# Encoder layer on one core: memory keys computed in halves between self-attention steps, the depthwise convolution on VectorE alone

## The chip, the cores and the metric

One core of a Trainium2 chip runs one program. The metric is device time in microseconds (us) of one execution; lower is better. The engines are TensorE (PE: matmuls and transposes), VectorE (DVE), ScalarE (ACT), GpSimd (POOL) and SyncE (SP), whose queue issues the loads. They work at the same time and wait for each other through semaphores.

## The reference

Two sequences, 256 and 512 tokens of width 1024, go through one encoder layer with shared weights, in fp32. What matters here is the first half:

```
h = layer_norm(x);  m = layer_norm(mem)                    # mem: 256 rows per sequence
q, k, v, a, gate = split(h @ w_in)                         # 512, 128, 128, 512, 512 columns
q, k = rope(rms_norm(q)), rope(rms_norm(k))                # per head of 64; 8 q heads, 2 kv heads
att  = softmax(q @ k.T / 8) @ v                            # within each sequence
u    = depthwise_conv31(a * sigmoid(gate)) + bias          # along tokens, 512 channels
u    = silu(layer_norm(u))                                 # over channels
h    = layer_norm(2**0.25 * h + concat(att, u) @ w_mix)
xa   = softmax((h @ w_cq) @ (m @ w_ck).T / 16) @ (m @ w_cv) @ w_co     # 4 heads of 256
h    = layer_norm(2**0.25 * h + xa)
```

A mixture of experts (32 experts, two per token) and a last norm follow; the change doesn't touch them.

## The kernel before

The 768 tokens lie as six tiles of 128 rows in `hres`; transposed, channels on partitions, in `hT`. Each engine has its own instruction list, written out by hand, and runs it in order. PSUM has eight banks; `plan_banks` gives every result its bank and its turn, in four banks for products ("mm"), two for transposes ("tr") and two for attention values ("pv"). `full` waits until a bank is written, `was_read` and `claim` until it is free again.

Weights come in slabs of 512 columns (2 MB) in the order of `weight_slabs`, through `ring`, which has three slots: slab n is loaded into slot n % 3 once the last product with slab n - 3 has been done (`load_slab`, L466). The order is a, g, q, kv, mix0, mix1, ck0, ck1, cv0, cv1, cq0, cq1, co0, co1.

- **Start.** Norm of the six tiles: VectorE takes statistics (`dve_stats`, L640), GpSimd the coefficients and the gain (`pool_coef`, `pool_gain`, L625), ScalarE the normalised rows (`act_hat`, L632), VectorE the bias (`dve_bias`, L657). TensorE transposes them (`rows_T`, L1577).
- **Convolution input.** `gates(c, s)` on TensorE makes a and gate for 128 channels c and sequence s, `gate(c, s)` on ScalarE evicts them, the sigmoid at L938.
- **Convolution.** The 256-token sequence: ScalarE scales one shifted copy per tap (L964), GpSimd adds it (L762). The 512-token sequence: VectorE alone, one instruction per tap (L1197), 31 taps for each of four groups of 128 channels. Mean and variance over channels are matmuls with a matrix of 1/512 (L1641); square root, reciprocal (L1216), scaling and Silu (L1017) follow, all before self-attention.
- **q, k, v.** Six tiles; squares and their sums on ScalarE, the factors on GpSimd (L746), the rotation (`rotate`, L666 to L682) on VectorE for four tiles and on GpSimd for two; TensorE transposes q and k (L1617).
- **Self-attention** is a loop of 24 steps (`STEPS`), each one query tile with two heads: eight steps with 256 keys, then sixteen with 512. Per step: scores (TensorE, L1707), maximum (VectorE, L1257), two exponentials with their sums (ScalarE, L1065), reciprocal (VectorE), normalisation of the two rows of probabilities (GpSimd, L778), transposes (TensorE, L1718), two copies out (VectorE, L1276). The values (L1730) come once per pair of heads, over all its query tiles.
- **Output projection and memory.** `product` (L1568) is eight matmuls. The mix products of six tiles (mix0 and mix1) are interleaved with norm 1, the transposes of the new rows, and the four memory tiles, which are loaded, normed and transposed here. Then come the keys of the memory (ck0, ck1: eight products of 512 columns), its values (cv0, cv1: eight products), the queries of cross-attention, cross-attention, and the rest.

## Time and profile before

| | us |
|---|---|
| median of 3 runs (lowest, highest) | 1152.93 (1151.47, 1153.18) |
| profiled execution | 1157.94 |
| its span, first to last instruction | 1156.2 |
| TensorE busy in the span | 978.5 (85%), mean granted clock 0.918 |
| VectorE, ScalarE, GpSimd busy | 427.1, 272.6, 424.6 |

A span is what the trace covers of one execution; "busy" counts instructions at work, not waits. The granted clock is the share of TensorE's full clock of 2.4 GHz; 0.50 is its lower level, 1.2 GHz. The chain of waits is followed back from the last instruction, at each step to what released it. L1568 is line 1568 of the kernel before. A matmul of fp32 leaves two records, so the counts of matmuls in the trace are twice those of the code.

### The profile page before, as it was taken

What the parts mean: (1) busy time and instruction counts of PE and PEld (TensorE: products, weight loads), DVE (VectorE), ACT (ScalarE), POOL (GpSimd) and SP (SyncE); (2) the same over time, 40 slices, a digit from 0 to 9 for tenths busy, and PEclk for the clock granted to TensorE, in tenths of its full rate; (3) what the DMA queues carried; (4) which work ended last, traced back from release to release, by engine and by line L of the source; (5) the groups of instructions that cost most, each with busy time, mean ns of one, the idle gap of its engine ahead of it and who ended that gap; (6) DMA issues with size and microseconds to landing.
All of it is one profiled execution on the core that took longest, in us unless ns stands there. A gap on an engine that the chain in (4) does not pass through costs nothing.

```text
span 1156.2 us, 10290 instructions
## 1 busy us (share of the span) xinstructions
PE 978.5 (85%) x3368; PEld 509.1 (44%) x3368; DVE 427.1 (37%) x702; ACT 272.6 (24%) x647; POOL 424.6 (37%) x496
## 2 busy tenths in 40 slices
PE   4899884757779998999999999995897999999910
PEld 3465442433334453444555754554643444444300
DVE  5199999566541432000000332225241112111156
ACT  2444564254421221001111430112010111111111
POOL 6688889727751542000000441120115121212037
PEclk9899997769989998999999999996598999999965
DMA  9201200120003014220420005006299799999652
GB/s 325 97 1 32 77 0 1 35 75 1 1 1 109 19 59 142 73 73 0 145 73 0 1 30 243 37 37 272 94 369 394 302 420 421 414 393 418 233 223 109
DMA packets 46234, 166.15 MB, mean 144 GB/s; under 512 B 8515, under 2 KB 13891, under 8 KB 33893
## 3 DMA queue, kind: packets, MB, share of 16 engines
q1 hardware_dynamic: 39460, 152.88, 34.3%
q0 software_dynamic: 6720, 12.60, 2.9%
q8 instruction: 28, 0.46, 0.2%
q14 instruction: 26, 0.20, 0.0%
HBM read 157.92 MB, written 18.03 MB: 152 GB/s over the span
## 4 chain that ended last, share of the span: by engine, by line
PE 68%; DVE 17%; POOL 8%; issue 4%; DMA 2%; ACT 1%; POOLq 0%; SPq 0%; DVEq 0%
PE ps L1568 34%; DVE cat L1197 11%; PE ps L1895 7%; PE ps L1924 7%; PE ps L1898 5%; POOL scr L778 4%; PE ps L1730 2%; PE ps L1654 2%; PE ps L1872 2%; PE ps L1679 2%; POOL hres L625 2%; PE ps L1577 1%; PE ps L1827 1%; PE ps L1718 1%; PE ps L1641 1%
## 5 line engine op out<-in xcount | busy, mean ns | idle before, releaser
L778 POOL TENSOR_SCALAR scr<-scr,rinv 128x256 f32<-128x256 f32 (+1 forms) x72 | 86.1, 1208 | 258.1 <-DVE rinv L1223 215.6
L1568 PE MATMUL ps<-ring,hT 128*128 128x512 f32 (+1 forms) x384 | 152.5, 558 | 23.3 <-ACT cat L990 12.9
L1568 PE MATMUL ps<-hT,ring 128*128 128x512 f32 (+1 forms) x512 | 170.7, 497 | 1.7 <-ACT hT L929 1.0
L1568 PEld LDWEIGHTS ps<-hT,ring 128*128 128x128 f32 x512 | 99.7, 195 | 71.4 <-issue 62.0
L1197 DVE SCALAR_TENSOR_TENSOR cat<-early,cpar,cat 128x512 f32<-128x512 f32 x120 | 127.5, 1063 | 4.2
L762 POOL TENSOR_TENSOR cat<-cat 128x256 f32<-128x256 f32 x120 | 114.1, 951 | 29.8 <-ACT cat L964 13.4
L1568 PEld LDWEIGHTS ps<-ring,hT 128*128 128x128 f32 x384 | 74.6, 196 | 98.8 <-issue 78.7
L1239 DVE TENSOR_REDUCE nmax<-ps 128x1 f32<-128x256 f32 x24 | 10.2, 424 | 215.3 <-PE ps L1654 215.3
L841 POOL DMA_INDIRECT pair_rows<-hT,sidx x22 | 22.0, 1001 | 182.9 <-DVE hT L1492 182.0
L1568 PE MATMUL ps<-ring,cat 128*128 128x512 f32 x192 | 83.8, 593 | 0.9 <-ACT cat L1055 0.9
L614 POOL TENSOR_SCALAR lnt<-mv 128x1 f32<-128x1 f32 x28 | 14.5, 518 | 161.0 <-DVE mv L642 160.0
L964 ACT ACTIVATE cat<-early,cpar 128x256 f32<-128x256 f32 x120 | 57.5, 506 | 43.2 <-POOL cat L762 42.7
L1924 PE MATMUL ps<-ring,memx 128*64 128x512 f32 (+1 forms) x144 | 59.9, 610 | 0.7 <-DVE memx L1482 0.7
L1568 PE MATMUL ps<-scr,ring 128*128 128x512 f32 x128 | 57.9, 616 | 0.7 <-ACT scr L1081 0.7
L1291 DVE SCALAR_TENSOR_TENSOR hres<-hres,ps 128x512 f32<-128x512 f32 x24 | 16.4, 685 | 109.3 <-PE ps L1568 109.3
L1482 DVE COPY memx<-ps 128x256 f32<-128x256 f32 x22 | 9.3, 424 | 128.4 <-PE ps L1907 124.6
L1568 PEld LDWEIGHTS ps<-ring,cat 128*128 128x128 f32 x192 | 35.9, 190 | 43.8 <-issue 43.8
L1568 PE MATMUL ps<-ring,scr 128*128 128x512 f32 x128 | 55.1, 592 | 0.0
L625 POOL TENSOR_TENSOR hres<-hres,gb 128x1024 f32<-128x1024 f32 x20 | 48.8, 2444 | 7.2 <-ACT hres L632 7.1
L632 ACT ACTIVATE hres<-hres,lnc 128x1024 f32<-128x1024 f32 x20 | 24.8, 1240 | 105.5 <-POOL lnc L616 105.3
L1718 PE MATMUL ps<-ident,scr 128*128 128x128 f32 x160 | 28.4, 304 | 21.3 <-POOL scr L778 20.3
L657 DVE TENSOR_TENSOR hres<-hres,gb 128x1024 f32<-128x1024 f32 x20 | 28.6, 1437 | 44.4 <-POOL hres L625 44.4
(267 smaller groups left out, 1447.2 us busy)
## 6 DMA issues: line engine op xcount, KB each, us to landing
ring<-w_down SPq DMA_DIRECT2D x16, 1024.0 KB
early<-w_gate SPq DMA_DIRECT2D x12, 1024.0 KB, 9.5
early<-w_up SPq DMA_DIRECT2D x12, 1024.0 KB, 13.0
ring<-w_gate SPq DMA_DIRECT2D x10, 1024.0 KB
ring<-w_up SPq DMA_DIRECT2D x10, 1024.0 KB
scr<-w_down SPq DMA_DIRECT2D x8, 1024.0 KB
cat<-w_down SPq DMA_DIRECT2D x8, 1024.0 KB
scr<-w_gate SPq DMA_DIRECT2D x5, 1024.0 KB
```

The source lines that it names most:

```text
L625: nc.gpsimd.tensor_tensor(rows, rows, g, ALU.mult).then_inc(ln_gain, 1)
L632: nc.scalar.activation(rows, rows, ACT.Identity, bias=lnc[:, n % 2, 1:2], scale=lnc[:, n % 2, 0:1]).then_inc(ln_hat, 1)
L657: nc.vector.tensor_tensor(rows, rows, b, ALU.add).then_inc(ln_done, 1)
L762: g.tensor_tensor(acc[:, c, 0:length], acc[:, c, 0:length], tap[n % NTAP], ALU.add).then_inc(conv_done[0], 1)
L778: g.tensor_scalar(prob[u % 4][:, 0:width], prob[u % 4][:, 0:width], rinv[:, u % 4:u % 4 + 1], None, ALU.mult).then_inc(prob_ready, 1)
L964: a.activation(tap[n % NTAP], src, ACT.Copy, scale=cpar[:, c, k:k + 1]).then_inc(taps_ready, 1)
L1197: ins = v.scalar_tensor_tensor(out=dst, in0=src, scalar=cpar[:, c, k:k + 1], in1=dst, op0=ALU.mult, op1=ALU.add)
L1568: last = t.matmul(out_of(bank), lhs(k), rhs(k), start=(k == 0), stop=(k == KC - 1))
L1718: last = t.transpose(bank[:, c * P:(c + 1) * P], prob[u % 4][:, c * P:(c + 1) * P], ident[:, :])
L1895: last = t.matmul(gu_out(64 * h, 64 * h + 64, b), xT[b][:, k, 64 * h:64 * h + 64], gu_of(n % GU_SLOTS, k), start=(k == 0), stop=(k == KC - 1))
L1898: last = t.matmul(gu_out(0, P, b), xT[b][:, k, :], gu_of(EXPERT_BLOCKS[j][1] % GU_SLOTS, k), start=(k == 0), stop=(k == KC - 1))
L1924: last = t.matmul(ps[h0:h1, 2 + n, :], hidT[b][:, k, h0:h1], w[:, k, n * 512:(n + 1) * 512], start=(k == 0), stop=(k == 1))
```

## The change

- **Memory.** Loads, norm and transposes of the four memory tiles move to the start, between the gates (`LN_M` now follows `LN_X`). The transposed memory lies in two halves, `mT[0]` and `mT[1]`.
- **Memory keys.** The eight key products are cut in halves of four matmuls (`memory_keys`), sixteen pieces, and one is issued in each of the steps listed in `CK_AT` of the self-attention loop. The slabs ck0 and ck1 are loaded ahead of mix0 and mix1.
- **Convolution.** VectorE alone, both sequences in one row of 798 columns with zeros between them (`AW`): 124 instructions. 108 stand ahead of the self-attention loop, 16 in its first four steps. Mean, variance, scaling and Silu move into the loop (`MEAN_AT`, `VAR_AT`).
- **Rotation.** Nine instructions on VectorE for all six tiles, with tables that hold the signs; two tiles ahead of the last channel group, two behind its first 15 taps, two in the loop.
- **Self-attention.** ScalarE normalises the probabilities (`self_normal`) in place of GpSimd, and does the second of the two copies (`self_turned`); the values come every second step for two query tiles (256 columns) in place of all at once.
- **Norm 1** is no longer interleaved with the memory's norms; GpSimd and VectorE take each tile's gain and bias before the next tile. Its gain and bias vectors have their own tile, `gb1`.

The core of the diff:

```diff
+            ("ck0", w_ck[:, 0:512]), ("ck1", w_ck[:, 512:1024]),
             ("mix0", w_mix[:, 0:512]), ("mix1", w_mix[:, 512:1024]),
-            ("ck0", w_ck[:, 0:512]), ("ck1", w_ck[:, 512:1024]),
             ("cv0", w_cv[:, 0:512]), ("cv1", w_cv[:, 512:1024]),
...
+QKV_ORDER = [("q", 0), ("q", 1), ("kv", 0), ("kv", 1)] + [(what, i) for i in range(2, NT) for what in ("q", "kv")]
 S_AHEAD = 3
 STEPS = len(SELF) // 2
-STEP_LAST = {SELF[2 * k][0]: k for k in range(STEPS)}
+GQ = 2 * P
+QKT_AT = {3: (2, 3), 6: (4, 5)}
+CK_AT = {k: n for n, k in enumerate((0, 1, 2, 3, 4, 5, 6, 7, 9, 11, 13, 15, 17, 19, 24, 25))}
+MEAN_AT, VAR_AT = 10, 14
...
+            for i in range(2):
+                sp.dma_start(mrow[i], mem[i * P:(i + 1) * P, :]).then_inc(mem_in[i], 16)
...
             for i in range(2, MT):
                 full(sp, ("mT", i - 2, 1))
                 sp.dma_start(mrow[i % 2], mem[i * P:(i + 1) * P, :]).then_inc(mem_in[i % 2], 16)
-            for n in range(7, 9):
+            for n in range(3, 8):
                 load_slab(n)
-            sp.wait_ge(ln_done, LN_1[-1] + 1)
+            sp.wait_ge(conv_out, CC)
+            for j in range(2):
+                sp.dma_start(gb1[:, j, :], bcast(lnp[2 + j])).then_inc(gb1_in, 16)
+            for n in range(8, 13):
+                load_slab(n)
             load_gb(2)
-            for n in range(9, len(w_slabs)):
+            for n in range(13, len(w_slabs)):
...
             norms(LN_X)
+            norms(LN_M[0:2])
...
+            norms(LN_M[2:MT])
...
+            for i in range(NT):
                 factors(i)
...
-            normalise(SELF, 0, True)
-            norms(sorted(LN_1 + LN_M))
-            normalise(CROSS, STEPS, False)
+            norms(LN_1, lag=0)
...
+            act_hat(act, LN_M[0])
             gate(0, 1)
...
+            act_hat(act, LN_M[1])
+            gate(1, 0)
+            for i in range(2):
+                mem_T(i)
+            gate(1, 1)
+            act_hat(act, LN_M[2])
+            act_hat(act, LN_M[3])
+            gate(2, 0)
+            for i in range(2, MT):
+                mem_T(i)
+            gate(2, 1)
+            for s in range(2):
+                gate(CC - 1, s)
...
+            def self_normal(k):
+                act.wait_ge(inv_ready, k + 1)
+                for u in (2 * k, 2 * k + 1):
+                    width = SELF[u][4]
+                    a.activation(sprob[u % 4][:, 0:width], sprob[u % 4][:, 0:width], ACT.Copy,
+                                 scale=rinv[:, u % 4:u % 4 + 1]).then_inc(prob_ready, 1)
+            def self_turned(k):
+                n, s, h, i, width = SELF[2 * k + 1]
+                key, m = ("sT", 2 * k + 1), width // P
+                bank = full(act, key)
...
+            qk_T(0)
+            qk_T(1)
             for k in range(STEPS + 3):
                 if k < STEPS:
                     self_exps(k)
...
+                if 1 <= k <= STEPS:
+                    self_normal(k - 1)
+                if 2 <= k < STEPS + 2:
+                    self_turned(k - 2)
+                if k >= 4 and k % 2 == 0:
+                    group_out((k - 4) // 2)
...
+                if CK_AT.get(k, 0) % 2 == 1:
+                    c = CK_AT[k] // 2
+                    if c == 0:
+                        act.wait_ge(u_ready, CC)
+                    bank = full(act, ("ck", c))
+                    a.activation(kmT[c], bank, ACT.Copy).then_inc(free(("ck", c)), 1)
+                if k == MEAN_AT + 1:
+                    for s, (t0, length) in enumerate(SEQS):
+                        was_read(act, ("mean", s))
...
+                if k == VAR_AT:
+                    for s in range(2):
+                        full(act, ("var", s))
+                    for s, (t0, length) in enumerate(SEQS):
+                        bank = full(act, ("var", s))
+                        a.activation(cstd[:, t0:t0 + length], bank[:, 0:length], ACT.Sqrt,
+                                     bias=epsv[:, 0:1]).then_inc(free(("var", s)), 1)
+                if VAR_AT + 3 <= k < VAR_AT + 3 + CC:
+                    c = k - VAR_AT - 3
+                    act.wait_ge(conv_norm, CC)
+                    a.activation(catv[:, CC + c, :], normed[:, c, :], ACT.Silu, bias=cpar[:, c, TAPS + 2:TAPS + 3],
+                                 scale=cpar[:, c, TAPS + 1:TAPS + 2]).then_inc(conv_out, 1)
...
+            def glu(c):
+                for s, (t0, length) in enumerate(SEQS):
+                    was_read(dve, ("a", c, s))
+                    was_read(dve, ("g", c, s))
+                    gated = upad[:, c, CONV_AT[s] + PAD:CONV_AT[s] + PAD + length]
+                    last = v.tensor_tensor(gated, gated, sig[:, c % 2, t0:t0 + length], ALU.mult)
+                last.then_inc(u_ready, 1)
+            def conv(c, k0, k1):
+                for k in range(k0, k1):
+                    src = upad[:, c, k:k + AW]
                     if k == 0:
...
+                        dve.wait_ge(u_ready, c + 1)
+                        ins = v.tensor_scalar(acc[:, c, :], src, cpar[:, c, 0:1], cpar[:, c, TAPS:TAPS + 1],
+                                              ALU.mult, ALU.add)
                     else:
...
+                        dve.wait_ge(conv_done, c * TAPS + k)
+                        ins = v.scalar_tensor_tensor(out=acc[:, c, :], in0=src, scalar=cpar[:, c, k:k + 1],
+                                                     in1=acc[:, c, :], op0=ALU.mult, op1=ALU.add)
+                    ins.then_inc(conv_done, 1)
+            def rotate(i):
+                pos = i - SEQS[TILES[i][0]][0] // P
+                r = raw[i].rearrange("p (h d) -> p h d", h=NQK)
+                dve.wait_ge(rqk_ready, i + 1)
+                rs = rqk[:, i, 1, :].rearrange("p (h a) -> p h a", a=1).to_broadcast([P, NQK, HD])
+                link(v.tensor_tensor(r, r, rs, ALU.mult))
+                A, B = rtmp
+                for tabx, h0, h1 in ((qtab, 0, HEADS), (ktab, HEADS, NQK)):
+                    last = v.tensor_tensor(A[:, h0:h1, :], r[:, h0:h1, :],
+                                           tabx[:, 0, pos:pos + 1, :].to_broadcast([P, h1 - h0, HD]), ALU.mult)
+                    for m in range(2):
+                        t = tabx[:, 1, pos:pos + 1, m:HD:2].to_broadcast([P, h1 - h0, HD // 2])
+                        last = v.tensor_tensor(B[:, h0:h1, m:HD:2], r[:, h0:h1, 1 - m:HD:2], t, ALU.mult)
+                link(last)
+                qo = raw[i][:, 0:HEADS * HD].rearrange("p (c a d) -> p a c d", c=PAIRS, a=2)
+                v.tensor_tensor(qo, A[:, 0:HEADS, :].rearrange("p (a c) d -> p a c d", a=2),
+                                B[:, 0:HEADS, :].rearrange("p (a c) d -> p a c d", a=2), ALU.add)
+                v.tensor_tensor(r[:, HEADS:NQK, :], A[:, HEADS:NQK, :], B[:, HEADS:NQK, :],
+                                ALU.add).then_inc(rot_ready, 1)
+            mem_rows(LN_M[0:2])
+            for n in LN_M[0:2]:
+                dve_bias(dve, n, link)
+            was_read(dve, "cpar")
+            glu(0)
+            conv(0, 0, 12)
+            mem_rows(LN_M[2:MT])
+            conv(0, 12, 18)
+            for n in LN_M[2:MT]:
+                dve_bias(dve, n, link)
+            conv(0, 18, 22)
+            glu(1)
+            conv(0, 22, TAPS)
+            conv(1, 0, 16)
+            glu(2)
+            conv(1, 16, TAPS)
+            conv(2, 0, 6)
+            glu(3)
+            conv(2, 6, TAPS)
             dve.wait_ge(tabs_ready, 1)
...
+            was_read(dve, ("mT", MT - 1, 1))
+            rotate(0)
+            rotate(1)
+            conv(3, 0, 15)
+            rotate(2)
+            rotate(3)
...
             for k in range(STEPS + 2):
                 if k < STEPS:
...
                     pair_inverse(k - 1)
                 if k >= 2:
                     pair_turned(k - 2)
+                if k < 4:
+                    conv(3, 15 + 4 * k, 19 + 4 * k)
+                elif k < 6:
+                    rotate(k)
+                if k == MEAN_AT + 1:
+                    for s, (_, length) in enumerate(SEQS):
+                        mean, at = full(dve, ("mean", s)), CONV_AT[s]
+                        for c in range(CC):
+                            last = v.tensor_tensor(acc[:, c, at:at + length], acc[:, c, at:at + length],
+                                                   mean[:, 0:length], ALU.subtract)
+                        last.then_inc(free(("mean", s)), 1)
+                if k == VAR_AT + 1:
+                    for s in range(2):
+                        was_read(dve, ("var", s))
+                    link(v.reciprocal(cstd, cstd))
+                if k == VAR_AT + 2:
+                    for s, (t0, length) in enumerate(SEQS):
+                        at = CONV_AT[s]
+                        for c in range(CC):
+                            last = v.tensor_tensor(normed[:, c, t0:t0 + length], acc[:, c, at:at + length],
+                                                   cstd[:, t0:t0 + length], ALU.mult)
+                            if s == 1:
+                                last.then_inc(conv_norm, 1)
...
+            for i, n in enumerate(LN_1):
+                if i >= 1:
+                    dve_bias(dve, LN_1[i - 1], link)
+                for j in range(2):
+                    residual(("mix", i, j), i, j).then_inc(free(("mix", i, j)), 1)
+                    was_read(dve, ("mix", i, j))
                 dve_stats(dve, n, link)
...
+            dve_bias(dve, LN_1[-1], link)
...
+            gates(1, 0)
+            for i in range(2):
+                rows_T("m", i, mrow[i], LN_M[i])
+            gates(1, 1)
+            gates(2, 0)
+            for i in range(2, MT):
+                rows_T("m", i, mrow[i % 2], LN_M[i])
+            gates(2, 1)
+            for s in range(2):
+                gates(CC - 1, s)
...
+            def memory_keys(n):
+                c, half = divmod(n, 2)
+                bank = claim(("ck", c)) if half == 0 else ps[:, place[("ck", c)][0], :]
+                w = slab(f"ck{c // 4}")
+                for k in range(4 * half, 4 * half + 4):
+                    last = t.matmul(bank, w[:, k, c % 4 * P:(c % 4 + 1) * P], mT[half][:, k % 4, :],
+                                    start=(k == 0), stop=(k == KC - 1))
+                if half == 1:
+                    done(("ck", c), last)
...
             for k in range(STEPS + 3):
+                if k == SEQS[0][1] // P * PAIRS:
+                    for key in ("qT", "kT", "kv"):
+                        was_read(pe, (key, NT - 1))
                 if k < STEPS:
                     self_scores(k)
                 if 2 <= k < STEPS + 2:
                     self_turn(k - 2)
...
+                if k >= 4 and k % 2 == 0:
+                    self_values((k - 4) // 2)
+                for i in QKT_AT.get(k, ()):
+                    qk_T(i)
+                if k in CK_AT:
+                    memory_keys(CK_AT[k])
+                if k == MEAN_AT:
+                    channel_mean("mean")
+                if k == VAR_AT:
+                    channel_mean("var")
```

## Rows read from the trace of the kernel before

**Rows 1.** Busy time by stage: start:end, length, busy us of each engine, granted clock, DMA share, GB/s.

```profile
58.70:196.40 137.70, 115.34 (x330) 64.46 (x329) 133.37 (x127) 70.05 (x222) 117.97 (x121) 0.93 0.08 23
196.40:249.30 52.90, 31.57 (x108) 20.18 (x106) 33.28 (x74) 20.44 (x64) 26.60 (x42) 0.78 0.15 40
249.30:347.77 98.47, 74.19 (x353) 34.58 (x353) 51.92 (x96) 37.34 (x105) 64.02 (x48) 0.88 0.03 11
347.77:442.10 94.33, 90.09 (x256) 43.11 (x257) 31.91 (x50) 19.71 (x26) 36.81 (x39) 0.99 0.24 84
```

**Rows 2.** The chain of waits, 340 to 660 us: start, us, what.

```profile
347.77 34.57 PE ps L1568 x80
...
421.05 0.87 PE ps L1577 x8
...
442.10 112.84 PE ps L1568 x256
```

**Rows 3.** DMA issues, 425 to 500 us: KB each, median us to landing.

```profile
ring<-w_cv SPq DMA_DIRECT2D x2, 2048.0 KB, 7.7
```

**Rows 4.** Timeline of DVE, ACT and POOL: start, us, instruction, idle before it.

```profile
23.20 1.24 DVE L657 TENSOR_TENSOR hres<-hres,gb 128x1024 f32<-128x1024 f32 x1 [2.24 <-POOL hres L625]
...
56.42 0.60 ACT L938 ACTIVATE scr<-ps 128x512 f32<-128x512 f32 x1 [6.27 <-PE ps L1568]
...
365.47 1.24 ACT L632 ACTIVATE hres<-hres,lnc 128x1024 f32<-128x1024 f32 x1 [17.96 <-POOL lnc L616]
...
366.86 2.36 POOL L625 TENSOR_TENSOR hres<-hres,gb 128x1024 f32<-128x1024 f32 x1
```

**Rows 5.** The convolution taps on DVE, one source line: duration in ns, min/median/max.

```profile
L1197 DVE SCALAR_TENSOR_TENSOR cat<-early,cpar,cat x120: 752/1097/1304, 58.7 to 195.4; 128x512 f32<-128x512 f32 x120
```

**Rows 6.** Timeline of DVE and POOL, 183 to 192 us.

```profile
183.53 8.39 DVE L1197 SCALAR_TENSOR_TENSOR cat<-early,cpar,cat 128x512 f32<-128x512 f32 x10
...
187.58 2.49 POOL L746 TENSOR_TENSOR rqk<-rqk,mhalf 128x10 f32<-128x10 f32 x1
```

**Rows 7.** Groups of DVE, 0 to 360 us, by shape: busy us, mean ns | idle before.

```profile
L1257 DVE TENSOR_REDUCE nmax<-ps 128x2 f32<-128x1024 f32 x16 | 19.5, 1218 | 12.2 <-PE ps L1707 12.2
...
L1216 DVE RECIPROCAL scr<-scr 128x768 f32<-128x768 f32 x1 | 5.0, 4952 | 0.5 <-ACT scr L1013 0.5
...
L650 DVE SCALAR_TENSOR_TENSOR hres<-hres,mv,gb 128x1024 f32<-128x1024 f32 x2 | 2.6, 1284 | 3.0 <-DMA gb<-lnp 3.0
L1209 DVE TENSOR_TENSOR cat<-cat,ps 128x512 f32<-128x512 f32 x4 | 2.5, 679 | 0.0
...
L666 DVE TENSOR_TENSOR ring<-ring,rqk 128x640 f32<-128x640 f32 x2 | 1.6, 820 | 5.6 <-POOL rqk L747 5.6
```

**Rows 8.** Timeline of PE in self-attention, 292 to 300 us.

```profile
293.03 3.65 PE L1730 MATMUL ps<-scr,early 128*64 128x512 f32 x16
296.61 1.13 PE L1707 MATMUL ps<-early 64*128 64x512 f32 x4
297.67 1.09 PE L1718 MATMUL ps<-ident,scr 128*128 128x128 f32 x8
```

**Rows 9.** Timeline of ACT, 231 to 301 us.

```profile
231.64 1.28 ACT L1013 ACT_TABLE_LOAD   x1
232.94 0.47 ACT L1013 ACTIVATE scr<-ps,epsv 128x256 f32<-128x256 f32 x1
...
242.90 3.78 ACT L1017 ACTIVATE cat<-cat,cpar 128x768 f32<-128x768 f32 x4 [4.78 <-DVE cat L1218]
...
299.12 0.69 ACT L1065 ACTIVATE scr<-ps,nmax 128x512 f32<-128x512 f32 x1 [1.80 <-DVE nmax L1257]
...
300.37 0.20 ACT L1065 ACTIVATION_READ_ACCUMULATOR scr<-ps,nmax 128x1 f32 x1
```

**Rows 10.** Busy time in two stretches of 4 us (columns as in rows 1).

```profile
316.00:320.00 4.00, 1.94 (x12) 1.14 (x12) 2.32 (x5) 2.18 (x7) 4.00 (x3) 1.00 0.00 0
...
336.00:340.00 4.00, 2.98 (x12) 1.80 (x10) 1.34 (x3) 0.00 (x0) 2.62 (x2) 0.50 0.00 0
```

515 lines of the change are left out of this document (186 added, 329 removed).

## The prediction, made before the changed kernel ran

> **What bounds the kernel now.** I read the busy time by stage first [rows 1]. From 58.7 to 196.4 us VectorE is busy 133 of 137.7 us (the taps of the 512-token sequence), while TensorE has 22 us to spare. From 196.4 to 347.8 us nothing is full: TensorE works 32 of 53 and then 74 of 98 us, at granted clocks of 0.78 and 0.88, and in the second of these stretches GpSimd works 64 of 98 us, normalising the softmax rows. From 347.8 us TensorE works 90 of 94 us. Second, the chain of waits [rows 2] is TensorE alone from there on, through output projection, memory keys and memory values. So TensorE's work after 347.8 us is paid at full price, and the same work before it is free as far as it fits into idle time. The sum needs two numbers: what leaves the full stretch, and how much later that stretch begins.
>
> **What leaves the full stretch.** A product is eight matmuls of 512 columns; the five products of the piece at 347.77 take 34.57 us (two records each matmul), so 6.9 us [rows 2]. Before, the time from 347.77 to the end of the value products is 94.33 (output projection, eight transposed tiles, a wait at the end) [rows 1] + 112.84 (keys and values) [rows 2] = 207.2 us. After, there remain 12 output products (82.8), four transposed tiles of 0.87 (3.5) [rows 2] and 8 value products (55.2): 141.5. The slab cv1 now goes into the slot of mix0, so its load is issued when the last mix0 product ends; TensorE then still has one transposed tile and one product, 7.8 us, and a slab takes 7.7 us to land [rows 3] plus about 0.5 us to issue: a wait of 0.5 to 2.5, I take 1. The key product's eight evictions and the memory norms leave this stretch too, but lay beside TensorE and are worth nothing. Gain: 207.2 - 142.5 = 64.7 us. Norm 1 becomes a serial loop on VectorE and GpSimd (residual, statistics, coefficients, hat, gain, bias: about 9.6 us by the durations in [rows 4]); a tile's two products take 13.8, so it stays hidden. Cross-attention and experts issue the same work; nothing is taken there.
>
> **The first tap comes later.** ScalarE ends the sigmoid of tile (0,1) at 57.0 us. Behind it in the new order stands the hat of memory tile 1 (1.24), then GpSimd's gain (2.36), VectorE's bias (1.24), and only then the gating of both sequences (about 0.4 more) [rows 4]: +5.3, first tap at 63.2 instead of 57.9. The memory loads join the queue behind the first two slabs, VectorE waits there until 57 us anyway: nothing. The rope tables and two memory gains now run on GpSimd beside the taps.
>
> **The taps.** A 512-wide tap takes 1097 ns in the median but 752 ns at least [rows 5]; the short ones are those from 183.5 us on, where GpSimd, until then adding taps, works on 10 numbers per partition [rows 6]. The same instruction 1024 wide takes 1284 [rows 7]. Between those, 798 columns take 752 + 286 x (1284-752)/512 = 1049 ns, and 0.036 to the next: 1.085 us. With GpSimd idle for nearly all of this stretch I take the fast price; at the slow ratio (1097/752) it would be 1.53 us. Before the loop: 104 taps (112.8), four openers (3.8), three more gatings (3.5), statistics and bias of two memory tiles (5.7), and four rotations. A rotation is nine instructions; by the 0.82 of its 640-wide scaling [rows 7] and the 0.4 to 0.7 that 256 to 512 columns cost, 4.3 us, so 17.2. GpSimd's tables and gains, some 10 us, slow taps by 3.5. Sum 146.5: the loop's first maximum at 209.8. TensorE has finished q, k and v by 186 (it starts them at about 124: the gates plus 4 us of transposes, then six tiles at 10.3), so VectorE is last here.
>
> **Steps 0 to 7 (256 keys).** VectorE: maximum 0.7, reciprocal 0.15, one copy 0.4 and four taps or one rotation (4.3): 5.6 us, six times less a bit at the start, 33: 242.8. TensorE per step: scores and transposes about 1.1, values 0.4, a key piece of four matmuls 3.45: 5.0, hidden. Steps 6 and 7 have no taps left, so TensorE's two key pieces set the pace: 11 us. TensorE idles from about 196 to 210 and restarts at half clock: 1.3. The exponentials of step 8 start at 255.
>
> **Steps 8 to 23 (512 keys).** Per step TensorE needs scores 1.07, transposes 1.09, values 1.8 every second step [rows 8], VectorE a maximum of 1.22 [rows 7], ScalarE two exponentials (1.45 with their sums) and now the normalisation: one activation of 512 columns takes 0.69 and 768 columns 3.78/4 = 0.945 [rows 9], so two take 1.4; and one copy, 0.6. The loop closes over two steps: exponentials 1.45, normalise 1.4, copy (frees the bank) 0.6, second half of the transposes 0.7, key piece 3.45, scores 1.1, maximum 1.3: 10.1 us for two steps when a key piece lies in them, 8.4 or ScalarE's 7.8 when none does. Thrown between: mean and variance sums on TensorE, 5.2 each; mean subtraction 4.4, reciprocal 4.95 [rows 7] and scaling 4.4 on VectorE; squares 3.0, roots 1.2, four Silus 4.0 and ten table loads on ScalarE. Walking the queues with these, the exponentials start at 265 (step 10), 278 (12, after the mean), 288 (14), 299 (15, variance and roots), 305 (16), 311 (17, reciprocal and scaling), 319, 326, 334, 341 (18 to 21, a Silu and two loads in each), 346 and 350 (23). So of some 45 us thrown in, 22 reach the path. Tail: exponentials and normalisation 2.9, transposes, values 1.8, two key pieces 6.9 and the last values, 16: 366. At half clock TensorE's work costs double. It kept full clock through the short waits of 316 to 320 us and ran at 0.50 behind the long one before 336 [rows 10]; beside the Silus its waits in the new order are 3 to 5 us, between the two. Nothing lost is one bound; the other is half clock from step 22 on to the mix, some 16 us of work that lies on the path. I take 6: transposes, values and scores of step 22 (3.9) and 2 in the tail. Mix begins at 372, 24 us later than before.
>
> Table loads: each took 1.28 us, and the root behind the one at 231.64 started at once, at 232.94 [rows 9]; that is what the walk uses. The Trainium skill, "ScalarE: Activation LUTs", section "What ACT_TABLE_LOAD costs", counts 1283 ns and a drain of about 1380 ns for every switch of table set, and advises calling functions set by set; this change interleaves Silu with Exp. By that, ten loads would cost some 14 us more; the trace of before shows no such drain, and the row decides.
>
> **The sum.** -64.7 + 24 = -41. The profiled execution took 1157.9 (span 1156.2), 5 above the median of 1152.9; I take the difference off the median: **1112 us**.
>
> **Rivals.** *The loop pipelines better (A):* clock held, key pieces under the pair's slack at 9.5: mix at 358 to 362, 1098 to 1102. For it: TensorE at full clock in most of self-attention. Against: one bank of each half for transposes. *ScalarE becomes the bound (B):* it has 1.45 + 1.4 + 0.6 of a 4 us step, plus loads, squares and roots; a pause behind each of ten loads as long as the load itself (13), 0.2 to 0.3 us of hand-over in each of 24 steps (5 to 7), or half clock to the end (10 more): 1120 to 1132. For the pause speaks only the drain that the Trainium skill's "ScalarE: Activation LUTs" adds to each switch; no row of before shows one. *Other side (C):* the 798-wide taps cost the slow price because something besides GpSimd's adding slows them. 120 x 0.48 = 58 us, all on VectorE's path: 1170. It decides from 0.34 us more per tap (1.39 us) on. For it: the median of the 120 taps is the slow price. Against: the ten fast ones beside busy ScalarE and TensorE. Halfway, it is also how the change could do nothing.
>
> **How the numbers follow.** My case 0.58 (1102 to 1120), A 0.15, B 0.20, C 0.07, of which 0.02 falls within 0.2% (about what a measurement of this kernel can tell from no change). Faster 0.93, same 0.02, slower 0.05. The range takes my case, A and B with their bounds: 1096 to 1132.
>
> **What would show it.** Taps 798 wide at about 1.05 us; the first maximum of self-attention near 210 us; key pieces between steps; eleven table loads in self-attention, 1.28 each with no gap behind; the output projection starting near 372; 142 us from there to the end of the value products, with a wait of about 1 us for cv1. Wrong if taps stay above 1.3 us, if ScalarE's steps run over 5.5 us without a key piece, or if the mix starts beyond 400.

## The result, and the profile after

The changed kernel takes 1106.07 us (median of 4 runs, 1104.72 to 1110.7) where the kernel before takes 1152.65 in runs beside it (1151.47 to 1153.18): 46.6 us less, a ratio of 0.9586 with a 95% interval of 0.9564 to 0.9608 (the two medians alone give 0.9596). The forecast was 1112, range 1096 to 1132. The profiled execution took 1107.07 with a span of 1105.4, 50.8 less than the span before; of the 5 us by which the profiled execution before lay above its median, only 1 is left here.

Busy time by stage, changed kernel (columns as in [rows 1]). The first row starts at 63.20, where the first tap was forecast; the others start where the loop's first exponential and the exponentials of steps 8, 16 and 23 do, and the last ends where the output projection starts:

```profile
63.20:201.90 138.70, 129.05 (x399) 73.54 (x397) 134.96 (x157) 30.95 (x159) 33.56 (x30) 0.99 0.18 57
201.90:251.66 49.76, 41.08 (x148) 19.11 (x148) 31.58 (x57) 21.05 (x67) 0.00 (x0) 0.86 0.01 4
...
251.66:301.71 50.05, 48.89 (x214) 24.30 (x212) 23.11 (x35) 32.74 (x69) 0.00 (x0) 1.00 0.14 39
301.71:345.82 44.11, 32.50 (x152) 16.25 (x148) 17.44 (x31) 38.22 (x67) 0.00 (x0) 0.88 0.07 24
345.82:363.69 17.87, 14.62 (x64) 7.49 (x65) 2.17 (x5) 6.82 (x14) 0.00 (x0) 0.90 0.08 19
```

Set beside [rows 1], self-attention is no longer a place where nothing is full. VectorE is full to 201.9 as before; then TensorE works 41 of 50 and 49 of 50 us; from step 16 to 23 (301.71 to 345.82) ScalarE is the full one, 38 of 44 us, and TensorE falls to 0.88 of its clock; in the tail everything waits in line.

The chain of waits of the changed kernel from the output projection on:

```profile
363.69 34.57 PE ps L1595 x80
...
442.97 61.97 PE ps L1595 x144
...
591.57 3.69 PE ps L1670 x16
```

And the start of cross-attention in the kernel before:

```profile
641.58 3.69 PE ps L1654 x16
```

The output projection starts at 363.69, 15.9 us later than before [rows 2]. From there to the end of the value products (442.97 + 61.97 = 504.94) are 141.25 us in place of 207.2: 65.9 less. Cross-attention starts at 591.57 in place of 641.58, 50.0 earlier, and the rest keeps that. So the result is 65.9 - 15.9 = 50.0 by the two profiles.

### The profile page after: what moved, and what is told of

The parts are those of the page before. It is cut to its first block, busy times and chain, and to the rows that moved or that the text cites. A ratio compares the mean times of both kernels' runs of the same rounds, so it can differ in the third digit from the quotient of the medians.

```text
span 1105.4 us, 10066 instructions
## 1 busy us (share of the span) xinstructions
PE 966.3 (87%) x3432; PEld 506.6 (46%) x3432; DVE 413.9 (37%) x680; ACT 260.2 (24%) x607; POOL 229.2 (21%) x296
## 4 chain that ended last, share of the span: by engine, by line
PE 61%; DVE 4%; ACT 3%; issue 3%; POOL 3%; DMA 1%; POOLq 0%; DVEq 0%
PE ps L1595 27%; PE ps L1942 8%; PE ps L1971 7%; PE ps L1945 5%; PE ps L1670 2%; PE ps L1919 2%; PE ps L1695 2%; PE ps L1874 1%; PE ps L1743 1%; POOL hres L644 1%; PE ps L1754 1%; PE ps L1604 1%; PE ps L1839 1%; DMA hT<-h_rows,gidx 1%; POOL slot_table L845 1%
## 5 line engine op out<-in xcount | busy, mean ns | idle before, releaser
L1595 PE MATMUL ps<-ring,hT 128*128 128x512 f32 (+1 forms) x384 | 145.6, 540 | 0.9 <-issue 0.9
L1182 DVE SCALAR_TENSOR_TENSOR cat<-early,cpar,cat 128x798 f32<-128x798 f32 x120 | 130.4, 1087 | 3.9
L651 ACT ACTIVATE hres<-hres,lnc 128x1024 f32<-128x1024 f32 x20 | 24.8, 1241 | 136.2 <-POOL lnc L635 135.9
L746 POOL TENSOR_SCALAR memx<-memx,rinv 128x256 f32<-128x256 f32 x24 | 22.1, 924 | 154.0 <-DVE rinv L1237 154.0
L1271 DVE TENSOR_REDUCE nmax<-ps 128x2 f32<-128x1024 f32 (+1 forms) x24 | 25.1, 1045 | 63.6 <-PE ps L1720 62.3
L1942 PE MATMUL ps<-early,hT 128*64 128x512 f32 x128 | 44.3, 627 | 0.8 <-ACT hT L1100 0.8
L1731 PE MATMUL ps<-ident,hT 128*128 128x128 f32 x160 | 26.4, 301 | 19.4 <-ACT hT L1015 17.7
L1945 PE MATMUL ps<-early,hT 128*128 128x512 f32 x96 | 42.5, 596 | 0.0
L1942 PE MATMUL ps<-ring,hT 128*64 128x512 f32 x96 | 42.3, 594 | 0.0
L1107 ACT ACTIVATE memx<-ps 128x256 f32<-128x256 f32 x22 | 8.4, 383 | 142.4 <-PE ps L1942 78.7
L1604 PE MATMUL ps<-ident,hres 128*128 128x128 f32 x144 | 22.5, 309 | 21.2 <-DVE hres L672 16.0
## 6 DMA issues: line engine op xcount, KB each, us to landing
ring<-w_down SPq DMA_DIRECT2D x16, 1024.0 KB, 16.9
early<-w_gate SPq DMA_DIRECT2D x12, 1024.0 KB, 10.6
```

The source lines that it names most:

```text
L651: nc.scalar.activation(rows, rows, ACT.Identity, bias=lnc[:, n % 2, 1:2], scale=lnc[:, n % 2, 0:1]).then_inc(ln_hat, 1)
L1182: ins = v.scalar_tensor_tensor(out=acc[:, c, :], in0=src, scalar=cpar[:, c, k:k + 1], in1=acc[:, c, :], op0=ALU.mult, op1=ALU.add)
L1271: v.tensor_reduce(nmax[:, c:c + 2], ps[:, b:b + 2, 0:width], AX.X, ALU.max, negate=True).then_inc(max_ready, 1)
L1595: last = t.matmul(out_of(bank), lhs(k), rhs(k), start=(k == 0), stop=(k == KC - 1))
L1604: last = t.transpose(bank[:, c * P:(c + 1) * P], rows[:, (4 * j + c) * P:(4 * j + c + 1) * P], ident[:, :])
L1731: last = t.transpose(bank[:, c * P:(c + 1) * P], sprob[u % 4][:, c * P:(c + 1) * P], ident[:, :])
```

## The experiments

Each experiment edits the changed kernel and is timed against the kernel before on its own chip. The third column is its ratio less 0.9586, times 1152.65: the difference from the changed kernel. Each ratio is uncertain by 0.002 to 0.003, so such a difference by 3 to 4 us. The span of the one profiled execution (1105.4 for the changed kernel) and the start of its output projection (363.69) stand beside it as a second witness. That witness varies too: the loop starts at 201.9 in the changed kernel, and at 202.7 to 203.0 in the profiles of e1, e2, e6 and e12 and at 205.7 in that of e8, whose edits all lie behind that start; and behind the projection, where only e4 differs, e6 and e9 took 2.5 and 1.8 us less.

| run | ratio (95%) | against the changed kernel, us | span | projection starts |
|---|---|---|---|---|
| e1 Silus in step 17 | 0.9532 (0.9514 to 0.9551) | -6.2 | 1100.5 | 358.48 |
| e12 Silus in step 18 | 0.9554 (0.9534 to 0.9574) | -3.7 | 1100.6 | 358.47 |
| e2 last key pieces earlier | 0.9504 (0.9484 to 0.9524) | -9.5 | 1096.5 | 354.99 |
| e3 hat first | 0.9554 (0.9532 to 0.9577) | -3.7 | 1101.2 | 359.92 |
| e4 keys after the projection | 0.9920 (0.9904 to 0.9935) | +38.5 | 1144.9 | 348.38 |
| e5 GpSimd busy beside taps | 0.9744 (0.9712 to 0.9776) | +18.2 | 1121.2 | 379.63 |
| e6 GpSimd normalises | 0.9527 (0.9497 to 0.9556) | -6.8 | 1096.3 | 357.08 |
| e7 taps split | 0.9608 (0.9577 to 0.9639) | +2.5 | 1106.0 | 364.62 |
| e8 TensorE filled | 0.9598 (0.9573 to 0.9623) | +1.4 | 1108.9 | 367.18 |
| e9 taps alternated | 0.9547 (0.9525 to 0.9568) | -4.5 | 1096.2 | 356.35 |
| e10 five edits | 0.9364 (0.9345 to 0.9384) | -25.6 | 1081.4 | 340.01 |
| e11 e10, normalisation split | 0.9385 (0.9370 to 0.9399) | -23.2 | 1079.1 | 336.76 |

My theory was that of the prediction: the key products leave the full stretch at full price and pay a part of it back in the loop. The rivals: the gain comes from the other parts, or the pieces are free in the loop.

**e4, the keys undone alone**

```diff
-CK_AT = {k: n for n, k in enumerate((0, 1, 2, ..., 24, 25))}
+CK_AT = {}
...
+            for n in range(2 * KC):      # behind the mix products
+                memory_keys(n)
             wv = [slab("cv0"), slab("cv1")]
```

> Memory keys undone alone: all eight key products behind the output projection again, slabs in the old order (mix before ck); convolution, rotation, normalisation and conv norm stay as changed. Nothing is left out. Theory (the prediction's steps 1, 4, 5): 55.2 us go back into the full stretch; the loop gives back 3 to 4 us in steps 6 and 7, 1.7 us for each of six pairs of steps, 7.3 in the tail, and perhaps 3 of half clock: 20 to 25 less there; so 30 to 35 us over the changed kernel, 1136 to 1141, with the output projection starting at 339 to 344. The keys are then worth some 33 of the 46.6 us and the rest of the change 13. Rival 1: the pieces were hidden but for the tail: 48 us more (1154, as slow as the kernel before: the keys are the whole gain). Rival 2: the loop pays the pieces in full: no more than 5 us over (the gain comes from the other parts).

38.5 us more, between theory and rival 1. The chain of waits of this kernel shows the keys back at full price:

```profile
348.38 34.57 PE ps L1600 x80
...
434.52 54.93 PE ps L1759 x128
489.45 54.95 PE ps L1600 x128
```

The other side is the start of the projection: 348.38, only 15.3 us earlier than with the pieces in the loop, not 20 to 25. Busy time of this kernel from the loop's first exponential to those of steps 8, 16 and 23, and to the projection:

```profile
202.02:241.88 39.86, 23.95 (x98) 13.00 (x100) 31.38 (x57) 18.86 (x63) 0.00 (x0) 0.60 0.00 0
241.88:293.38 51.50, 41.42 (x186) 21.19 (x182) 23.31 (x35) 32.24 (x67) 0.00 (x0) 0.90 0.00 1
293.38:336.47 43.09, 27.71 (x136) 14.08 (x132) 17.25 (x31) 37.77 (x65) 0.00 (x0) 0.80 0.08 25
336.47:348.38 11.91, 7.77 (x49) 4.69 (x49) 2.17 (x5) 6.22 (x13) 0.00 (x0) 0.86 0.00 1
```

Beside the changed kernel's 49.8, 50.1, 44.1 and 17.9 us, the eight pieces of steps 0 to 8 cost 9.9 us, the two of steps 16 to 23 cost 1.0 and the two of the tail 6.0. The four of steps 8 to 16 cost nothing: without them that stage is 1.5 us longer, though the theory had put 1.7 us on each pair of steps. In their place TensorE waits there, in step 11 for VectorE's subtraction of the mean, and does what stands behind the wait more slowly (these values take 1.95 us at full clock):

```profile
259.32 1.12 PE L1725 MATMUL ps<-early 64*128 64x512 f32 x2 [2.36 <-DVE cat L1311]
...
265.61 3.32 PE L1748 MATMUL ps<-hT,early 128*64 128x256 f32 x16
```

With less to do, TensorE had a lower granted clock in every stage: 0.60, 0.90, 0.80 and 0.86, against 0.86, 1.00, 0.88 and 0.90 with the pieces. How much of each stage the clock made up, and how much the other engines, is not shown. So, with the rest of the change in place, the keys are worth some 38 of the 46.6 us, and all the other parts together about 8.

**e6, normalisation undone alone**

```diff
-                if 1 <= k <= STEPS:
-                    self_normal(k - 1)
...
+            for k in range(STEPS):       # GpSimd
+                pool.wait_ge(inv_ready, k + 1)
+                for u in (2 * k, 2 * k + 1): ...  # g.tensor_scalar(..., rinv, None, ALU.mult)
```

> Normalisation of self-attention undone alone: GpSimd multiplies the rows by the reciprocals again, as in the kernel before (1562 ns for 512 columns, 924 for 256, against 715 and some 450 on ScalarE). Nothing is left out. Theory: a pair's normalisation is on the loop of two steps, so 3.12 instead of 1.32 us and a hand-over of 0.2 cost 2 us in each of eight pairs of steps, and some 0.5 in the steps of 256 keys where TensorE is not full; ScalarE gets back 1.3 us in each of the four Silu steps, which it paces: +16 + 2 - 5, so 8 to 15 us over the changed kernel, 1114 to 1121. Rival 1: ScalarE is the bound of the whole loop, and relief of it wins: 5 us or more less. Rival 2: GpSimd works beside, no change.

The theory falls: 6.8 us less, not 8 to 15 more. Stages of this kernel, from step 8 to 16 and from 16 to 23:

```profile
251.38:301.09 49.71, 48.79 (x214) 24.28 (x212) 23.10 (x35) 23.61 (x53) 23.58 (x16) 1.00 0.14 39
301.09:339.06 37.97, 30.14 (x152) 14.76 (x148) 17.68 (x31) 29.61 (x52) 21.99 (x14) 0.96 0.09 28
```

Steps 8 to 16 take 49.7 us whether a pair of rows is normalised in 1.3 us by ScalarE or in 3.1 by GpSimd. TensorE is busy all but 1 us in both, and the longer normalisation is hidden there. Steps 16 to 23 shrink from 44.1 to 38.0: ScalarE set the pace there, and it is relieved of 1.3 us a step. Putting the normalisation on ScalarE is thus a part of the change that cost time, as rival 1 had it, but in the last third of the loop only.

**e1 and e12, the Silus in one step**

```diff
-                if VAR_AT + 3 <= k < VAR_AT + 3 + CC:
-                    c = k - VAR_AT - 3
+                if k == 17:              # e12: 18
                     act.wait_ge(conv_norm, CC)
+                    for c in range(CC):
...
```

> The four Silus run together in step 17 instead of one each in steps 17 to 20; nothing is left out. Two of the eight table loads that the Silus bring remain, so ScalarE loses 6 x 1.28 = 7.7 us of work. Theory: in the changed kernel's profile ScalarE alone paces steps 17 to 21 (the chain of waits goes from table load to Silu to table load to exponential without a break), so most of it comes back: 5 to 7 us less than the 1106.1 of the changed kernel, about 1100. Rival 1: TensorE's key pieces of steps 17 and 19 take over as the pace at once: 0 to 2 us less. Rival 2: each change of table set costs a drain beside the load, which the profile doesn't show as such; then six changes less are worth 6 x 2.66 = 16 us (1090).

> The four Silus in step 18 instead of step 17, everything else as in the changed kernel; nothing is left out. With them in step 17, TensorE stood for 4.96 us behind them and came back at half clock: the key piece of step 19 took 5.75 instead of 3.6 us, and steps 19 to 20 were 8.9 us apart. Theory: in step 18 the Silus stand beside a step whose transposes and key piece TensorE can do without waiting for ScalarE, so the wait is shorter, the piece takes 3.6 us, and the 2.2 us and some more come back: 7 to 10 us below the changed kernel, 1096 to 1099. Rival: the wait only moves; 5 to 6 us below, as in step 17.

What they go at, the chain of waits of the changed kernel in step 17 and 18:

```profile
310.42 0.29 ACT L1063
310.70 1.01 issue
311.71 1.03 ACT cat L1063
312.75 1.28 ACT L1006
314.08 0.55 issue
314.63 0.86 ACT hT L1006 x3
```

That is a table load, a Silu, a table load and the exponential, with nothing between them. e1 came out as the theory had it: six loads less are worth 6.2 us (4.9 by the spans). e12 was to win more, and did not; its projection starts at the same time to 0.01 us. TensorE in e1, then in e12 (timelines, behind the Silus):

```profile
319.99 2.12 PE L1732 MATMUL ps<-ident,hT 128*128 128x128 f32 x8 [4.96 <-ACT hT L1016]
321.90 5.75 PE L1755 MATMUL ps<-scr,ring 128*128 128x512 f32 x8
```

```profile
324.43 2.12 PE L1732 MATMUL ps<-ident,hT 128*128 128x128 f32 x8 [3.68 <-ACT hT L1016]
326.48 3.48 PE L1744 MATMUL ps<-hT,early 128*64 128x256 f32 x16
```

In step 17 the key piece behind the wait took 5.75 in place of 3.6; in step 18 the piece was through before, and the transposes and values behind the wait took 2.12 and 3.48 in place of 1.09 and 1.95. The wait moved, and what came behind it paid for it, as the rival said. The two ratios lie too close to be told apart.

**e2, the last two key pieces in steps 21 and 23**

```diff
-... 17, 19, 24, 25))}
+... 17, 19, 21, 23))}
```

> The last two key pieces go into steps 21 and 23 instead of 24 and 25; nothing is left out. Theory: behind the last exponentials everything is serial (3.90 and 3.44 us of key pieces lie on the chain there), while TensorE is idle for 2 to 4 us in each of steps 20 to 23 behind ScalarE; so the tail loses 7.3 us and the steps gain some 1 to 2: 5 to 6 us less than the changed kernel, about 1101. Rival: the pieces push scores and transposes of steps 21 to 23 back by as much as they free at the end: 0 to 2 us less.

9.5 us less, more than expected. Its last two stages (exponentials of steps 16 to 23, then to the projection):

```profile
302.26:344.37 42.11, 35.28 (x161) 17.07 (x158) 17.23 (x31) 38.01 (x66) 0.00 (x0) 0.92 0.08 26
344.37:354.99 10.62, 9.06 (x57) 5.29 (x55) 2.18 (x5) 6.82 (x14) 0.00 (x0) 1.00 0.55 198
```

The tail went from 17.9 to 10.6, the 7.3 of two pieces. The steps did not pay for it: they became 2 us shorter, with the granted clock at 0.92 and 1.00 in place of 0.88 and 0.90. That the clock is what shortened them agrees with e4, but was not tried by itself.

**e3, the hat of memory tile 1 ahead of gate (0,1)**

```diff
             act_hat(act, LN_M[0])
-            gate(0, 1)
             act_hat(act, LN_M[1])
+            gate(0, 1)
```

> ScalarE's hat of memory tile 1 goes ahead of the gate (0,1); nothing is left out. Theory: the bias of that tile, at 57.05 us, is what VectorE waits for ahead of the first gating and tap; the sigmoid it needs is ready at 53.3. So first tap some 4 to 5 us earlier (56 instead of 60.7), and since VectorE is full from there to the loop's first maximum, the same 4 to 5 off the total, about 1102. Rival: TensorE, which ends its q, k, v products at 187 us, or the transposes behind the rotations, takes over and the loop starts as late as before: nothing off.

The first tap starts at 55.69 in place of 60.69, the loop 3.3 earlier, the total 3.7 lower. VectorE gave some of the 5 us back at 80.77: it now waits 3.99 us for GpSimd's gain of memory tile 2, and its first bias, beside the next gain, takes 3.28 us in place of 1.2. The changed kernel lost 4.1 us at the same place, in two taps beside these gains (see e5).

**e5, GpSimd busy beside the taps**

```diff
+            spare = qT[:, 0, 0:256]
+            link(g.memset(spare, 0.0))
+            for n in range(60):
+                link(g.tensor_tensor(spare, spare, spare, ALU.add))
             for i in range(NT):
                 factors(i)
```

> GpSimd gets 60 adds of 128x256 on a tile that nobody reads, behind the memory gains and ahead of the rotation factors: work without use, nothing is left out. In the kernel before, GpSimd's adds of this shape took 968 ns, so it is busy for some 58 us from about 84 us on; the factors are needed at 171 us, so nothing waits for them. Theory (the prediction's step 3): GpSimd's adding is what makes VectorE's taps slow (1097 against 752 ns, a ratio of 1.46); the taps beside it take 1.53 us instead of 1.05, VectorE loses 58 x (1 - 1/1.46) = 18 us and the total rises by as much, to about 1124. Rival (C): something else made them slow; the taps stay at 1.05 and the total within 2 us of the changed kernel.

18.2 us more, as the theory had it, but not by its arithmetic. The taps of this kernel that start from 100 to 139.5 us (min/median/max), and GpSimd's adds:

```profile
L1186 DVE SCALAR_TENSOR_TENSOR cat<-early,cpar,cat x29: 1279/1281/1395, 100.0 to 139.5; 128x798 f32<-128x798 f32 x29
```

```profile
L742 POOL TENSOR_TENSOR early<-early 128x256 f32<-128x256 f32 x60 | 71.1, 1185 | 4.7
```

A tap beside an add takes 1.28 us, 0.23 over the 1.05 without, not 1.53: the surcharge is not a ratio. And the adds ran longer than I assumed, 71 us in place of 58. By the profiles the loop starts 16.9 us later: 12.0 us are in the taps, 3.9 in the gatings, biases and openers beside the adds, and 1.1 came ahead of the first tap, where nothing was edited.

The Trainium skill, "SBUF — State Buffer", section "SBUF: two separate sides", calls the port pair that VectorE and GpSimd share an exclusive lock that is held for a whole instruction, so that the other blocks fully. The adds show contention, but not that much of it: between 84 and 156 us VectorE was busy 70.4 and GpSimd 67.7 of 72 us. A tap came every 1.31 us (15 in 19.72) and an add every 1.26 (60 in 75.75); in turns, a tap of 1.05 and an add of 0.97 (its time in the kernel before, beside shorter taps) would need 2.02. Longer GpSimd instructions come nearer to it. In the changed kernel two taps stand beside GpSimd's gains of memory tiles 2 and 3, 1024 columns wide (such a gain takes 2.35 us where VectorE is idle):

```profile
78.88 3.25 DVE L1182 SCALAR_TENSOR_TENSOR cat<-early,cpar,cat 128x798 f32<-128x798 f32 x1
82.17 3.01 DVE L1182 SCALAR_TENSOR_TENSOR cat<-early,cpar,cat 128x798 f32<-128x798 f32 x1
```

```profile
78.94 5.40 POOL L644 TENSOR_TENSOR memx<-memx,scr 128x1024 f32<-128x1024 f32 x2
```

These two taps took 2.2 and 2.0 us more than a tap alone, nearly the length of a gain. Why short adds cost a tap so much less is not shown.

**e7 and e9, the taps split and alternated**

```diff
-                    src = upad[:, c, k:k + AW]
...
+                    for s, (_, length) in enumerate(SEQS):      # e7: 256 and 512 columns, one behind the other
```

```diff
-            conv(1, 16, TAPS)
-            conv(2, 0, 6)
+            def conv_both(c, k0, k1):                           # e9
+                for k in range(k0, k1):
+                    conv(c, k, k + 1)
+                    conv(c + 1, k - k0, k - k0 + 1)
+            conv_both(1, 16, TAPS)
```

> Each 798-wide tap becomes two, 512 and 256 wide, still all on VectorE; the 30 columns between the sequences, whose values nobody reads, are left out. Theory (the prediction's price of a tap): a tap is a fixed part of some 0.22 us and 1.04 ns a column (752 ns for 512, 1284 for 1024), so 0.75 + 0.49 against 1.05: 0.19 us more for each of 104 taps ahead of the loop, 20 us, and 2 to 3 in the first steps: 1126 to 1129. Rival: the time goes by columns alone; then 30 columns less make it 4 us faster.

> The taps keep their width of 798 columns, but 80 of the 104 taps ahead of the loop are issued alternately for two channel tiles (0 and 1, 1 and 2, 2 and 3), so that each stands behind one that it doesn't read; 89 taps of the old order's 89 single ones in tiles 0 to 2 and all of tile 3 are still done, nothing is left out. Theory, from the split taps (763 and 495 ns, yet 30 of them in 15.95 us): of a tap's 1.083 us some 0.25 is latency that only a tap on the same row pays; alternated, a tap takes about 0.96, and VectorE is 80 x 0.12 = 10 us earlier at the loop (192 instead of 202), the total 9 to 10 us below the changed kernel: 1096 to 1098. Rival 1: the time is all throughput, the split gained by its 30 columns less: 0. Rival 2: TensorE, which ends q, k, v at 187, or the factors take over: no more than 5 us.

(In e9 all 124 instructions are done; 80 of them alternate.) The theory of e7 falls, and so does its rival: the 2.5 us more are within the uncertainty of no change. Its groups, mean ns of each, and then the timelines of VectorE in e7, in the changed kernel and in e9:

```profile
L1184 DVE SCALAR_TENSOR_TENSOR cat<-early,cpar,cat 128x512 f32<-128x512 f32 x120 | 91.6, 763 | 0.0
L1184 DVE SCALAR_TENSOR_TENSOR cat<-early,cpar,cat 128x256 f32<-128x256 f32 x120 | 59.5, 495 | 0.0
```

```profile
123.20 15.95 DVE L1184 SCALAR_TENSOR_TENSOR cat<-early,cpar,cat 128x256 f32<-128x256 f32 x30
```

```profile
121.09 16.24 DVE L1182 SCALAR_TENSOR_TENSOR cat<-early,cpar,cat 128x798 f32<-128x798 f32 x15
```

```profile
121.56 26.97 DVE L1184 SCALAR_TENSOR_TENSOR cat<-early,cpar,cat 128x798 f32<-128x798 f32 x28
```

Two pieces cost 763 + 495 = 1258 ns by their durations, yet thirty of them take 15.95 us, 1.06 for a pair, because a piece starts before the one ahead has ended; it waits only for the piece before that. The 798-wide tap waits for the tap just ahead and comes every 1.083 us. Alternated between two channel tiles at full width it comes every 0.963 us (26.97/28). So some 0.12 us of a tap is paid only by an instruction that waits for the one just ahead, whose result it reads. In e9 the loop starts at 195.46 in place of 201.91, with VectorE still the last to be ready. The 80 x 0.12 us would be 9.6; of these 0.9 went ahead of the first tap and 1.0 to one more tap that now lies ahead of the loop. The total falls by 4.5 us, 7.3 by the start of the projection: less than the 9 to 10 expected.

**e8, TensorE filled**

```diff
+                if k == 2:               # and fill(4) behind key piece 1
+                    fill(6)              # t.matmul(ps[:, 7, 0:384], ident, mT[0][:, 0, 0:384])
                 if 2 <= k < STEPS + 2:
                     self_turn(k - 2)
```

> TensorE gets ten matmuls of 384 columns without use in its waits of steps 1 and 2 (behind key piece 1 and ahead of the first transposes), into a bank that the next key piece clears: work without use, nothing is left out. Theory: those two waits (3.6 and 4.3 us) are why TensorE stands at a granted clock of 0.50 from 205 to 210 us, and key pieces 2 and 3 take 5.75 and 5.30 instead of 3.6 us; TensorE paces steps 3 to 7, so filling the waits gives back 3 to 4 us: about 1102. Rival 1: those steps are VectorE's; nothing changes. Rival 2: the filling itself holds up the transposes; 1 to 3 us more.

Nothing measurable. What it goes at, TensorE in the changed kernel, and then in e8 (timelines):

```profile
208.28 1.08 PE L1731 MATMUL ps<-ident,hT 128*128 128x128 f32 x4 [4.30 <-ACT hT L1015]
209.16 5.75 PE L1754 MATMUL ps<-gb,ring 128*128 128x512 f32 x8
...
220.09 5.30 PE L1754 MATMUL ps<-scr,ring 128*128 128x512 f32 x8
```

```profile
212.71 3.60 PE L1754 MATMUL ps<-gb,ring 128*128 128x512 f32 x8
...
221.10 0.63 PE L1651 MATMUL ps<-ident,scr 128*128 128x128 f32 x4 [3.13 <-DVE hT L1288]
...
224.41 5.94 PE L1754 MATMUL ps<-scr,ring 128*128 128x512 f32 x8
```

Piece 2 ran at full clock, 3.60. TensorE was then ahead by that much, stood longer for VectorE (3.13 in place of 1.18 us), and piece 3 took 5.94 at the low clock. Up to step 3 VectorE sets the pace: the transposes of q and k in that step wait for its copy (L1288), and time given to TensorE ahead of them comes back as that wait. (In this profile the loop started 3.8 us later, ahead of the edit; steps 0 to 4 took 26.1 in place of 25.0 us, steps 4 to 8 24.8 in both.)

**e10 and e11, edits put together.** e10 has the edits of e2, e3, e6, e9 and e12 at once. e11 has them too, but gives the first row of each step to ScalarE and the second to GpSimd:

```diff
-                for u in (2 * k, 2 * k + 1):      # ScalarE
+                for u in (2 * k,):
...
+                for u in (2 * k + 1,):            # GpSimd
```

> Five edits at once: last key pieces in steps 21 and 23, hat of memory tile 1 first, taps alternated, GpSimd normalises self-attention, the four Silus in step 18 (where a key piece and transposes of the next step stand beside them). Nothing is left out. Theory: the tail loses 7 to 9, VectorE reaches the loop 10 + 4 us earlier but TensorE's products hold it at about 192 (10 to 11), relief of ScalarE 6 to 9, of which the Silus' share is mostly the same time as GpSimd's: 24 to 28 us below the changed kernel, about 1080. Rival: the edits free the same time, and TensorE's own work (41 of 50 and 47 of 48 us busy in steps 0 to 16) is the floor: 15 us or less.

> As the combined kernel, but the two normalisations of a step lie on two engines: the first on ScalarE (0.7 us), the second on GpSimd (1.57). Nothing is left out. Theory: a step's normalisation then takes 1.6 us instead of 3.1 (GpSimd) and ScalarE carries 0.7 more; in the last steps, which no key piece fills, the chain through exponential, normalisation and transposes is shorter by 1.5 a step: 2 to 4 us below the combined kernel. Rival: TensorE is the floor of steps 8 to 23 there, and it makes no difference.

e10 takes 1081.13 us (1078.09 to 1083.1) and beats both kernels; the 25.6 us below the changed kernel are what the theory gave. Busy time of its loop, from the first exponential to those of steps 10 and 16 and to the projection:

```profile
193.82:251.02 57.20, 50.69 (x188) 23.16 (x188) 34.99 (x62) 19.23 (x64) 21.52 (x20) 0.94 0.22 58
251.02:292.32 41.30, 40.85 (x183) 20.66 (x178) 19.87 (x29) 19.86 (x41) 18.61 (x12) 1.00 0.00 1
292.32:340.01 47.69, 42.45 (x216) 21.67 (x213) 19.73 (x34) 26.06 (x56) 28.13 (x18) 0.96 0.19 67
```

TensorE is busy 134 of 146 us. e11 adds nothing that can be measured: its interval overlaps that of e10, and from the first exponential to the projection its loop takes 145.6 us in place of 146.2. That fits its rival, by which TensorE is the floor there; e4 warns that a busy TensorE alone does not prove it.

## Why the prediction was right, point by point

- **What leaves the full stretch: right.** 65.9 us gained where 64.7 were forecast. The wait of 1 us for cv1 did not come: value products take cv0 and cv1 in turn, so one more product of 6.9 us lay ahead of the first that needs cv1, and the walk left it out. Norm 1 stayed hidden.
- **The first tap: the mechanism right, 3.3 us too late.** The first tap of a group also adds the bias (I call it the opener). It came at 57.85 before and was forecast for 63.2; it came at 59.94:

```profile
57.85 0.83 DVE L1194 TENSOR_SCALAR cat<-early,cpar 128x512 f32<-128x512 f32 x1
```

```profile
59.94 0.71 DVE L1178 TENSOR_SCALAR cat<-early,cpar 128x798 f32<-128x798 f32 x1
```

Hat at 53.22, gain 54.59, bias 57.05, gating 58.36: the chain as written. The sigmoid it hangs on ended at 53.3, not 57.0; TensorE began those products at 38.72.
- **The taps: right.** 104 taps took 117.0 us; forecast 112.8 and 3.5 for contention, of which 4.1 came in the two taps beside the gains. A tap is 1.05 us in the median, 1.083 to the next; the fast price was right. e5 shows that GpSimd's adding makes taps slow, though at 1.28 and not 1.53: at that surcharge rival C would have cost half of its price. A rotation took 3.5 us, not 4.3, and an opener 0.7, not 0.95; these and the early start are most of why the loop's first maximum came at 201.2, 8.6 us early.
- **Steps 0 to 7: too cheap by 5 us.** From the first maximum to step 8 took 50.5 in place of 45.2 us. Two steps stretch it: 3 to 4 lasted 10.1 us and 6 to 7 lasted 8.7. They are those in which TensorE also transposes q and k of two tiles, 2.8 us (217.31 to 220.09) and 2.9 us (238.07 to 240.96), and VectorE waits 4.8 and 7.6 us for the scores behind them. The walk has no term for these transposes. TensorE in the changed kernel where they begin:

```profile
217.31 0.63 PE L1651 MATMUL ps<-ident,scr 128*128 128x128 f32 x4 [1.18 <-DVE hT L1288]
...
238.07 0.66 PE L1651 MATMUL ps<-ident,scr 128*128 128x128 f32 x4
```

The rest is half clock, put at 1.3: key pieces 2 and 3 took 5.75 and 5.30 in place of 3.6. Piece 2 is mostly hidden behind VectorE's taps, and e8 shows that filling TensorE's waits does not give it back.
- **Steps 8 to 23: the time right, 94.2 for 95, the reason wrong.** The forecast closed the loop over ScalarE's exponentials and normalisation, 10.1 us a pair with a key piece and 8.4 without. Up to step 16 a normalisation more than twice as long is hidden (e6), and taking the pieces out gains nothing (e4). TensorE is busy there 48.9 of 50 us, but what sets that length is open. From step 16 on ScalarE is the pace: rival B's mechanism is there, inside the time I had forecast. That the sum of these steps fits is luck.
- **Tail and half clock: 4 us too dear.** 17.9 where 16 and 6 were put. The low clock did come (in step 21 transposes took 2.12 and values 3.63 us, and step 22 lasted 6.9 us without a key piece or a Silu), but most of it lay in steps whose time was right already.
- **Table loads: right.** Eleven of 1283 ns, and the next activation starts at once (310.42 + 1.28, then 311.71). The drain that the Trainium skill's "ScalarE: Activation LUTs" adds in "What ACT_TABLE_LOAD costs" does not show: e1 took six loads away and gained 6.2 us, 4.9 by the spans. Loads alone are 7.7; with the drain it would be 16.
- **The sum.** The projection started 15.9 us later than before, not 24: -8.6, +5.3, -0.8 and -4.1 by the points above. Against -41 the profiles show -50, the medians -46.6: the profiled execution lay 5 us above its median before and 1 after. So the mechanism of the gain was right, and the errors of the loop in part cancelled: the time came nearer than its terms.

## What to carry to other kernels

Look for the stretch where one engine is full and for another, later or earlier, where it idles; moving work between them is worth its full price less what the receiving stretch then pays. That price differs from place to place in one and the same loop: 16 half products cost 9.9 us in steps 0 to 8, nothing in steps 8 to 16, 1.0 in steps 16 to 23 and 6.0 in the tail. A busy engine does not show it: TensorE was nearly full in steps 8 to 16, and taking the work out again made them no shorter. Before a busy engine is given more, see what pace each part of the loop keeps: the normalisation was free on GpSimd, and on ScalarE it cost 7 us. A time that comes out right does not prove the model behind it; undoing one part alone tests it.

## What the runs showed of the hardware

- A VectorE instruction that waits for the one just ahead, whose result it reads, pays for it: 798-wide taps come every 1.083 us on one row, every 0.963 alternated on two.
- Taps of 1.05 us beside GpSimd's adds of 256 columns take 1.28 in the median (1.28 to 1.40), while the adds go on at 1.19. Two taps beside GpSimd's gains of 1024 columns took 3.25 and 3.01.
- Work for TensorE in a loop that others pace is cheaper than its duration: some 55 us of key products in the loop delayed the projection by 15.3 us. With them TensorE's granted clock was 0.86, 1.00, 0.88 and 0.90 in the four stages of the loop, without them 0.60, 0.90, 0.80 and 0.86.
